# Gate projection in PSUM banks 0 to 3 with its bias rows inside the expert branch, and the second half's normalised rows scaled on VectorE, in a transformer block with 32 experts

## The reference

```python
h = layer_norm_2(DEEPNORM_ALPHA * h + y @ w_out[i], ln1_g[i], ln1_b[i])
m = moe(h, w_router[i], b_router[i], w_up[i], b_up[i], w_down[i], b_down[i])
h = layer_norm_2(DEEPNORM_ALPHA * h + m, ln2_g[i], ln2_b[i])
h = h + jax.nn.sigmoid(h @ w_ple_gate[i] + b_ple_gate[i]) * (p[i] @ w_ple[i])
```

## Time and profile before

| what | value |
|---|---|
| median of the three runs | 2494.17 us |
| time of the profiled execution | 2496.79 us |
| its span, first to last instruction | 2495.0 us |
| mean granted TensorE clock | 0.991 |
| TensorE busy (matmul) | 2438.0 us, 98% |
| VectorE, ScalarE, GpSimd busy | 1106.1, 829.3 and 201.0 us |
| DMA | 665.16 MB, mean 267 GB/s |

### The profile page before, as it was taken

How to read it: one execution, slowest core, us unless ns; L and a number is a source line. 1 busy time by engine, 2 the same in 40 slices (tenths; PEclk the granted TensorE clock), 3 DMA queues, 4 the chain that set the end, 5 groups by cost and what they waited for, 6 DMA issues and landing times. The chain is left out here.

```text
span 2495.0 us, 36318 instructions
## 1 busy us (share of the span) xinstructions
PE 2438.0 (98%) x15029; PEld 1792.1 (72%) x15029; DVE 1106.1 (44%) x1439; ACT 829.3 (33%) x961; POOL 201.0 (8%) x96
## 2 busy tenths in 40 slices
PE   9999999999999999999999999999999999999998
PEld 8999988999999998899998954444444444444443
DVE  4557766644644867654568651221112121111123
ACT  4344344433433434433346411222112221211121
POOL 0002402200200340120020010000000000000000
PEclk9999999999999999999999998999999999999998
DMA  7665454565555545456545465999999999999992
GB/s 242 211 203 168 137 186 146 172 204 170 186 189 185 169 138 184 135 189 204 166 161 161 163 240 244 428 428 429 428 428 428 429 428 428 429 429 429 429 428 114
DMA packets 215595, 665.16 MB, mean 267 GB/s; under 512 B 9873, under 2 KB 164239, under 8 KB 190912
## 3 DMA queue, kind: packets, MB, share of 16 engines
q1 hardware_dynamic: 215488, 663.57, 69.9%
HBM read 662.50 MB, written 1.05 MB: 266 GB/s over the span
## 5 line engine op out<-in xcount | busy, mean ns | idle before, releaser
L607 PE MATMUL ps<-ring_halves 128*128 128x256 f32 x5984 | 754.2, 284 | 0.0
L607 PEld LDWEIGHTS ps<-ring_halves 128*128 128x128 f32 x5984 | 735.1, 192 | 3.6 <-issue 0.6
L1832 DVE TENSOR_TENSOR ring_halves<-ring,ring_halves 128x2048 fp32r<-128x2048 f32 x206 | 511.5, 2491 | 361.2 <-ACT ring_halves L1350 361.1
L1350 ACT CAST ring_halves<-ring 128x2048 fp32r<-128x2048 f32 x206 | 391.2, 1903 | 276.3 <-PE ps L607 141.7
L1189 PE MATMUL ps<-ring,work 128*64 128x512 f32 x2048 | 451.3, 595 | 22.8 <-DMA ring<-in_w_up_dram 22.1
L1338 ACT COPY work<-ps 128x512 f32<-128x512 f32 x190 | 109.7, 586 | 840.9 <-PE ps L1189 389.8
L1189 PEld LDWEIGHTS ps<-ring,work 128*64 128x64 f32 x2048 | 145.4, 137 | 322.7 <-issue 268.7
L2334 DVE TENSOR_SCALAR work<-work 128x128 f32<-128x128 f32 x64 | 19.3, 344 | 611.6 <-PE ps L1189 611.6
L618 PE MATMUL ps<-ring_halves,work_halves 128*128 128x512 f32 x1184 | 288.4, 391 | 0.0
L618 PEld LDWEIGHTS ps<-ring_halves,work_halves 128*128 128x128 f32 x1184 | 219.7, 188 | 44.4 <-issue 0.5
L1227 PE MATMUL ps<-ring,work 128*64 128x512 f32 x1024 | 226.8, 595 | 2.0
(11 more groups left out here) (256 smaller groups left out, 1735.5 us busy)
## 6 DMA issues: line engine op xcount, KB each, us to landing
ring<-in_w_up_dram SPq DMA_DIRECT2D x128, 2048.0 KB, 23.7
ring<-in_w_down_dram SPq DMA_DIRECT2D x64, 2048.0 KB, 19.3
ring<-in_w_in_dram SPq DMA_DIRECT2D x52, 1024.0 KB, 5.2
ring<-in_ffn_gate_dram SPq DMA_DIRECT2D x44, 1024.0 KB, 5.3
ring<-in_ffn_up_dram SPq DMA_DIRECT2D x44, 1024.0 KB, 5.3
ring<-in_ffn_down_dram SPq DMA_DIRECT2D x44, 1024.0 KB, 4.9
ring<-in_w_out_dram SPq DMA_DIRECT2D x12, 1024.0 KB, 4.9
ring<-in_ca_k_dram SPq DMA_DIRECT2D x8, 1024.0 KB, 5.2
```

The lines of the kernel that those rows point to most:

```text
L607: mm = pe.matmul(ps[:, bank, pt * T:pt * T + T], wt[:, o:o + P], x[:, k, :], start=(k == 0 and n == 0), stop=(k == DT - 1 and n == 2))
L1350: nc.scalar.copy(high_of(name)[:], ring[:, s, :]).then_inc(hi_done.add(name), 1)
L1832: v.tensor_tensor(ring_halves[s][:], ring[:, s, :], high_of(name)[:].bitcast(F32), ALU.subtract)\
```

## The change

Two things are changed.

**Routing.** `best(0)` moves from between the normalisation and the evacuation of half 1 to behind the evacuation. GpSimd scales the rows of half 0 only and signals `("h", ("A",))` after them. VectorE scales half 1: the product by g ("scaled") between best(0) and best(1), the sum with b ("rows") behind the softmax weights and ahead of `pos`. TensorE waits for "rows" in `few()`, and does the gather for expert 0 first and `expert_biases` behind it. `gT` goes into bank 1 in place of bank 2. SyncE waits for "rows" before it loads the last norm's parameters, which overwrite those of this one.

**End.** The gate projection uses the banks 0 to 3 in place of 4 to 7. Its four bias matmuls stand behind the last combine inside each branch of the fork, and the fork's offsets become 0 since those banks are then open. The last norm's transposes use the banks 4 to 7.

```diff
         def t_bank(tag, t):
-            first = 2 * t if tag[0] != 1 else 2 - 2 * t
+            first = 4 + 2 * t if tag[0] == "B" else 2 * t if tag[0] != 1 else 2 - 2 * t
...
                 sp.wait_ge(h_ready.sem, h_ready.at(("h", before_ln(tag))))
+                if tag[0] == "B":
+                    sp.wait_ge(dve_done.sem, dve_done.at("rows"))
...
-            open_bank(2, "gT")
+            open_bank(1, "gT")
...
             def few():
-                expert_biases("few")
                 pe.wait_ge(h_ready.sem, h_ready.at(("h", ("A",))))
+                pe.wait_ge(dve_done.sem, dve_done.at("rows"))
                 pe.wait_ge(sel_ready.sem, sel_ready.at("sel0"))
                 gather("xg0")
+                expert_biases("few")
...
+            def gate_biases(branch):
+                row = arrived("bpg")
+                for b in range(4):
+                    open_bank(b, ("pg", branch))
+                    o = 512 * (b % 2)
+                    mm = pe.matmul(ps[:, b, :], ones[0:1, :], ring[0:1, row, o:o + 512], start=True, stop=False)
+                mm.then_inc(used[row].sem, 1)
...
             with pe.If(n < CAP + 1):
                 few()
-                fork.end("few", [1] * 4 + [0] * 5)
+                gate_biases("few")
+                fork.end("few", [0] * 9)
...
-            gate_bias(0)
             transposes(last, 0, hn)
-            gate_bias(1).then_inc(used[row].sem, 1)
             turned_copied(last, 0)
...
                 done(v.memset(w(YS, 512), 0.0), "clear")
-                link(best(0))
             ln(("A",), ("ln1_g_2", "ln1_b_2"), 0, ALPHA2, first_half)
+            link(best(0))
+            mine(("hn", ("A",), 1))
+            dve.wait_ge(lnp_in.sem, lnp_in.at((("A",), 1)))
+            done(v.tensor_tensor(h[:, 1, :], hn[:, 1, :], w(LNP["A"], D), ALU.mult), "scaled")
             done(best(1), "chosen")
...
             done(ins, "gates")
+            mine("scaled")
+            done(v.tensor_tensor(h[:, 1, :], h[:, 1, :], w(LNP["A"] + D, D), ALU.add), "rows")
...
-                for t in range(TT):
+                for t in range(1 if tag[0] == "A" else TT):
                     pool.wait_ge(dve_done.sem, dve_done.at(("hn", tag, t)))
                     link(g.tensor_tensor(h[:, t, :], hn[:, t, :], w(at, D), ALU.mult))
                     ins = g.tensor_tensor(h[:, t, :], h[:, t, :], w(at + D, D), ALU.add)
-                    if t == 1:
+                    if t == 1 or tag[0] == "A":
                         ins.then_inc(h_ready.add(("h", tag)), 1)
```

More of the change, by code:

```diff
@@ L1119, in _ @@
             embedding(1, 1)
-            open_bank(2, "gT")
+            open_bank(1, "gT")
             pe.wait_ge(dve_done.sem, dve_done.at("gates"))
             for t in range(TT):
-                mm = pe.transpose(ps[0:32, 2, t * P:t * P + P], work[:, GATES + t * 32:GATES + t * 32 + 32], ident[:])
+                mm = pe.transpose(ps[0:32, 1, t * P:t * P + P], work[:, GATES + t * 32:GATES + t * 32 + 32], ident[:])
             full(mm, "gT")
             def expert_biases(branch):
-                evacuated(2, "gT")
+                evacuated(1, "gT")
                 for t in range(TT):
@@ L1282, in _ @@
                 few()
-                fork.end("few", [1] * 4 + [0] * 5)
+                gate_biases("few")
+                fork.end("few", [0] * 9)
             with pe.Else():
                 many()
-                fork.end("many", [1] * 4 + [0] * 5)
+                gate_biases("many")
+                fork.end("many", [0] * 9)
             fork.join("experts done")
             last = ("B",)
[L1290 to L1297, removed]
             def gate_part(t, half, j):
@@ L1301, in gate_part @@
                 for kk in range(2):
-                    mm = pe.matmul(ps[:, 4 + 2 * t + half, :], hT[:, 2 * j + kk, t * P:t * P + P],
+                    mm = pe.matmul(ps[:, 2 * t + half, :], hT[:, 2 * j + kk, t * P:t * P + P],
                                    ring[:, s, kk * D + half * 512:kk * D + half * 512 + 512],
@@ L1737, in _ @@
             pe_group("gT")
-            nc.scalar.copy(work[0:32, GT:GT + T], ps[0:32, 2, 0:T]).then_inc(emptied[2].sem, 1)
+            nc.scalar.copy(work[0:32, GT:GT + T], ps[0:32, 1, 0:T]).then_inc(emptied[1].sem, 1)
             embedded(1, 1)
@@ L1788, in gate @@
             def gate(t, half):
-                b = 4 + 2 * t + half
-                nc.scalar.activation(w(SGB + 512 * (b - 4), 512), ps[:, b, :], ACT.Sigmoid).then_inc(emptied[b].sem, 1)
+                b = 2 * t + half
+                nc.scalar.activation(w(SGB + 512 * b, 512), ps[:, b, :], ACT.Sigmoid).then_inc(emptied[b].sem, 1)
             pe_group(("pg", 0))
@@ L2446, in _ @@
                     b = 2 * t + half
-                    bank_empty(4 + b, ("pg", t))
+                    bank_empty(b, "experts done")
                     x = w(SGB + 512 * b, 512)
```

## The result

Four runs of the changed kernel took 2474.55 to 2480.97 us, median 2475.57; four of the kernel before had a median of 2495.53. The ratio is 0.9927, 95% interval 0.9911 to 0.9942: by it the change is worth 18 us; the two medians lie 20.0 apart. A second set of four runs gave 2477.28 us and a ratio of 0.994 (0.9923 to 0.9956). The forecast was 2475.7.

What follows compares the result with a forecast made beforehand. DMA's weight stream was taken as the bound from expert 0 on, so earlier first slots count fully: routing 14.1 plus end 4.4 made 18.5 us, 2475.7 us against the median 2494.17; range 2470.0 to 2484.0.

Steps and rivals of the forecast that it cites:

- rival E: Expert loop: shifted code makes TensorE stall at every return to the loop's start, 2562 us; chance 0.03.
- The chain on VectorE: Routing: VectorE's steps, from the evacuation to select(0), end last, so the gather starts at about 1493.5.
- The fork behind `most`: Routing: TensorE's fork before the gather costs between nothing and 2.6 us; nothing was taken.
- No fall at all: Routing: everything at 2.4 GHz, first slots released at 1504.8 against 1520.57, 15.8 us earlier.
- The toll of the clock: Routing: one short fall to 1.2 GHz around the biases, 1.7 us allowed, so 14.1 us of gain remain.
- The bound of 13.6 us: Routing: a low-clock stretch as long as the one at the end would cost 6.8 us, leaving 9.0.
- Rival A: Routing: the clock falls early all the same, say from the small router and `pos` matmuls, 2480.8 us; chance 0.20.
- The end: After the last combine: biases hidden by the fork's exit, gate_part earlier, a low clock costing 2.7 us; gain 4.4 us.
- The other bound: End: with the low clock kept to 2463.7, the gain is 2.5 us.
- C as a rival: End: the way out of the fork begins behind the biases, the end gives 1.3 us, 2478.8 us; chance 0.12.
- Rival B: End: no fall of the clock if the biases count as work, 2472.1 us; chance 0.14.
- The reason for the move to VectorE: Routing: half 1 on VectorE costs 2.4 us on the chain, bought with undisturbed best(0) and the new order.

Runs made afterwards that it cites:

- the end alone: Only the end part of the change, with the routing as in the kernel before: 2488.26 us, ratio 0.9981.
- the experiment behind the fork: The changed kernel with the gate's bias matmuls behind the fork, ahead of the transposes: 2483.23 us, ratio 0.9963.
- the experiment gives 1.4 us: The changed kernel with half 1's rows made on GpSimd again, best(0) still behind the evacuation: 2477.54 us, ratio 0.993.
- the last kernel: The changed kernel with both bias sets over 128 rows, rows on GpSimd, and VectorE's last evacuation before half 1's statistics: 2473.97 us, ratio 0.9919.
- the one with both over 128 rows: The changed kernel with the down biases and the gate's biases contracted over 128 rows: 2473.54 us, ratio 0.9918.

## Why the prediction was right

**Total and bound.** 2475.7 was forecast; 2475.57 and 2477.28 were measured. That the stream of weights would carry every microsecond of the routing to the end held in every kernel, with 925.9 to 926.6 us from the first issue to the last combine. No expert got longer, so rival E is out as well.

**The chain on VectorE.** Forecast from the rows: evacuation with no delay, gather 12.7 us after N. Measured 12.17. Router(1), best(), the two row operations and the gather had the durations taken. The fork behind `most` cost TensorE nothing that shows: ahead of the gather TensorE stood idle for 0.77 us, until line 2330 was done, within the 1.4 that I had left. With the rows on GpSimd, where TensorE was the last, the gather even followed `gT` without a gap.

**No fall at all** was priced at 15.8 us of gain. The one execution with 32-row biases and no fall had N to I of 23.57, 16.2 less than before.

**The toll of the clock** was the soft term: 1.7 us allowed, with 6.8 as the bound. The first profile paid about 5 (28.64 against 23.57), the second 1.7 (25.23). The place was right, around the down biases. The size is not one number but a draw, and the 14.1 us forecast stand against 11.1 and 14.5 measured. These figures are against one execution of the kernel before; the end alone, with the same routing, would put them 2.2 lower. The bound of 13.6 us comes out as 13.0 from the two times that it names; the clock had fallen at 2450.05, within the gap, so the stretch was indeed 13.7 us long. The first issue at 1510.24 is later than the 1505 to 1507 named (in the second profile it was 1503.28), and one sign that I had called wrong, a clock of 0.5 in the biases, was there, though not in the gather. Rival A, a fall ahead of the gather, came in neither profile of the changed kernel; it came when best(0) went between, and with the biases put first it began with the gather.

**Where the gain in the routing lies.** Of the stage before, 27.3 us ran at 1.2 GHz, of the stage after 10.2 and 3.4. At half their length, as if all of it lay on the path, they cost 13.7, 5.1 and 1.7 us. By this estimate the clock makes up 8.5 of the 11.1 us and 12.0 of the 14.5, and the shorter chain 2.6 in both. The prediction contains most of this without naming it, as it prices TensorE's steps at 2.4 GHz. In both executions that have the 4.32 us gap, before and end only, a fall came within it; in the kernels with no gap ahead of router(1) none came ahead of the down biases or, where those are missing or wide, of I.

**The end.** 4.4 us forecast, 5.4 and 4.5 measured. (The other bound, with the low clock kept to 2463.7, comes out as 2.6 and not 2.5.) The biases ran beside the exit, C as a rival fell, and the experiment behind the fork shows what it would have cost. gate_part was forecast 7.9 us after C and came after 8.1. Rival B was wrong even with 128 rows: a fall of 3.4 us remained. What I held against it, the gap of 2.62 us that also lowered the clock, was weaker than it looked: the same gap lowered it in 7 executions of 14.

**The reason for the move to VectorE** was weighed right in its cost (2.4 us of VectorE) and too kindly in its use. I booked an undisturbed best(0) as its gain; the experiment gives 1.4 us for that and so a small net loss of 0.6; the last kernel against the one with both over 128 rows shows the same 0.63, 22.80 against 23.43. What paid was the new order of best(0) and evacuation and the clock that it kept up. What the order of gather and biases adds rests on one profile.

**In the sum**, the first profile's 11.1 and 5.4 make 16.5, and with N 0.8 later 15.7, which is the span's 15.8. The agreement of the median with the forecast to 0.1 us is closer than the terms deserve.

## What to carry to other kernels

Where a saturated stream of transfers starts behind a short chain of small steps, that chain is worth its full length, and marks inside the trace (here N, first issue, last combine) measure it far more sharply than totals, which scatter by 4 us for reasons ahead of it. The stretches at 1.2 GHz vary from one execution to the next even there, so note the clock beside each distance. Where the order is free, put small matmuls over few rows behind the work on the path (one profile shows it here). Work that needs nothing from the other side of a branch goes ahead of the branch's exit. Moving an operation to a neighbour engine to free a port is only worth it if the operation is shorter than the hold-up that it ends.

## What the runs showed of the hardware

- The granted clock fell from 2.4 to 1.2 GHz while TensorE was busy without a gap, in matmuls over 32 rows or 0.1 us behind them, in nine executions of ten; the same work over 128 rows with zeros kept it up, in three executions of three. I had expected idle gaps to be the usual cause. Falls come with them too, but not always: near 1487.5, within the 4.32 us gap before; close behind the same gap of 2.6 us in 7 executions of 14; 2.5 us behind one of 1.35 us in one kernel. Gaps of 0.64 to 0.88 us were followed by none in five kernels.
- A stretch at 1.2 GHz lasted 3.4, 6.8, 10.2, 13.7 or 17.1 us, and in the same kernel not the same from one execution to the next.
- Behind the last combine TensorE stood 3.67 to 4.01 us at the way out of the branch in three kernels, with nothing that released it; with the eight bias instructions (3.7 us) ahead of the exit it was ready for the transposes before `hn` was.
- VectorE's small instructions, 0.17 and 0.24 us alone, took 1.54 and 2.39 us beside GpSimd and ended 0.03 us behind its instruction, while others beside it weren't held up.
- Up to the end of the same normalisation, the same kernel took 1478.05 and 1481.60 us, and all kernels together 1477.87 to 1481.60. A fall of the clock near 1365 us goes with the longer times; whether it is the cause was not tried.
